# S5 states stored by place in a block, the S5 recurrence on VectorE alone, and two gate items moved into the RWKV groups

## What is computed

```python
def rwkv7_scan(r, w, k, v, kk, a):
    def step(state, xs):
        r_t, w_t, k_t, v_t, kk_t, a_t = xs
        sa = jnp.einsum('bhvk,bhk->bhv', state, -kk_t)
        state = (state * w_t[:, :, None, :] + sa[..., None] * (kk_t * a_t)[:, :, None, :]
                 + v_t[..., None] * k_t[:, :, None, :])
        return state, jnp.einsum('bhvk,bhk->bhv', state, r_t)
...
    # s5_branch: 64 groups of 64 complex states, s_t = a * s_(t-1) + bu_t
    bu_re = jnp.einsum('gpc,blgc->blgp', bb_re, ug)
    bu_im = jnp.einsum('gpc,blgc->blgp', bb_im, ug)
    _, _, s_re, s_im = lax.associative_scan(combine, (a_re_t, a_im_t, bu_re, bu_im), axis=1)
    y = jnp.einsum('gcp,blgp->blgc', c_re, s_re) - jnp.einsum('gcp,blgp->blgc', c_im, s_im)
...
    # second_block
    gates = jax.nn.sigmoid(gate_logits.astype(jnp.float32).reshape(bsz, seq, N_BRANCH, D_MODEL)
                           + gate_b[i].astype(jnp.float32))
    merged = jnp.sum(gates * branch_proj, axis=2)
```

## Time and profile before

| | us |
|---|---|
| median of 3 runs | 4223.11 (4216.96 to 4227.99) |
| the profiled execution | 4227.98 |
| its span | 4226.1 |
| TensorE busy | 3696.7 (87%) |
| VectorE busy | 2460.8 (58%) |
| ScalarE busy | 1190.7 (28%) |
| GpSimd busy | 477.2 (11%) |
| mean granted TensorE clock | 0.937 |

### The profile page before, as it was taken

The page is one execution under the profiler, slowest core; times in us unless marked ns, Lnnn a source line. Parts: engine busy times, 40 slices in busy tenths (PEclk is TensorE's granted clock), DMA queues, the critical chain, the costliest instruction groups (busy, mean ns, idle before and its releaser), DMA issues. The chain is left out here.

```text
span 4226.1 us, 47590 instructions
## 1 busy us (share of the span) xinstructions
PE 3696.7 (87%) x19527; PEld 2904.3 (69%) x19527; DVE 2460.8 (58%) x3027; ACT 1190.7 (28%) x1252; POOL 477.2 (11%) x713
## 2 busy tenths in 40 slices
PE   2599868899999999999999699787977777999888
PEld 1475547789999999888888587486835774444336
DVE  7665668579777644555555545655445445993224
ACT  1223223334444443434334332213311002000003
POOL 1011101000100000000000000020001110992000
PEclk9999869899999999999999898898988888999999
DMA  7866327356777676766667452105451005553553
GB/s 269 301 225 201 117 74 301 138 187 199 259 252 251 247 248 219 242 241 243 245 240 247 150 199 87 45 1 209 159 181 35 1 6 150 145 159 119 184 206 122
DMA packets 246293, 750.71 MB, mean 178 GB/s; under 512 B 31264, under 2 KB 42612, under 8 KB 210368
## 3 DMA queue, kind: packets, MB, share of 16 engines
q1 hardware_dynamic: 217008, 645.44, 44.5%
q0 software_dynamic: 29072, 102.25, 6.9%
HBM read 692.29 MB, written 54.75 MB: 177 GB/s over the span
## 5 line engine op out<-in xcount | busy, mean ns | idle before, releaser
L1860 DVE TENSOR_TENSOR expert_w_low<-expert_w,expert_w_high 128x2048 fp32r<-128x2048 f32 x256 | 586.6, 2292 | 556.2 <-ACT expert_w_high L2152 555.7
L2152 ACT ACTIVATE expert_w_high<-expert_w 128x2048 fp32r<-128x2048 f32 x256 | 489.4, 1912 | 433.7 <-PE bank L2141 410.5
L2082 PE MATMUL bank<-h_high,expert_w_high 128*128 128x256 f32 x2048 | 583.7, 285 | 9.3 <-DVE expert_w_low L1860 8.2
L2083 PE MATMUL bank<-h_low,expert_w_high 128*128 128x256 f32 x2048 | 580.5, 283 | 0.0
L2084 PE MATMUL bank<-h_high,expert_w_low 128*128 128x256 f32 x2048 | 580.4, 283 | 0.0
L281 DVE TENSOR_TENSOR weights_low<-weights,weights_high 128x1024 fp32r<-128x1024 f32 (+2 forms) x280 | 328.8, 1176 | 324.4 <-ACT weights_high L268 322.0
L268 ACT ACTIVATE weights_high<-weights 128x1024 fp32r<-128x1024 f32 (+2 forms) x280 | 284.9, 1021 | 678.5 <-PE bank L305 424.1
L2082 PEld LDWEIGHTS bank<-h_high,expert_w_high 128*128 128x128 f32 x2048 | 394.0, 192 | 10.2 <-DVE expert_w_low L1860 8.8
L2139 PE MATMUL bank<-expert_w_high,gated_acts_high 128*128 128x512 f32 x1024 | 398.3, 389 | 0.0
L2140 PE MATMUL bank<-expert_w_low,gated_acts_high 128*128 128x512 f32 x1024 | 398.3, 389 | 0.0
L2141 PE MATMUL bank<-expert_w_high,gated_acts_low 128*128 128x512 f32 x1024 | 398.3, 389 | 0.0
(11 more groups left out here) (670 smaller groups left out, 5803.5 us busy)
## 6 DMA issues: line engine op xcount, KB each, us to landing
expert_w<-in_peer_u_dram SPq DMA_DIRECT2D x128, 1024.0 KB, 5.9
expert_w<-in_peer_v_dram SPq DMA_DIRECT2D x128, 1024.0 KB, 5.0
weights<-in_w_in_dram SPq DMA_DIRECT2D x84, 1024.0 KB, 9.8
s_gates_w<-in_w_in_dram SPq DMA_DIRECT2D x80, 512.0 KB, 3.6
ada_ring<-in_ada_w_dram SPq DMA_DIRECT2D x64, 512.0 KB, 5.0
weights<-in_w_out_dram SPq DMA_DIRECT2D x32, 1024.0 KB, 11.6
weights<-in_w_branch_dram SPq DMA_DIRECT2D x48, 512.0 KB, 6.0
mod_mid_ring<-in_ada_w_dram POOLq DMA_DIRECT2D x32, 512.0 KB, 6.5
```

The costliest lines, as they stand in the source:

```text
L1860: dve.tensor_tensor(wl[:, n % RING, :], w_sb[:, n % RING, :], wh[:, n % RING, :], ALU.subtract).then_inc(wl_ready, 1)
L2082: pe.matmul(o, uh[:, b, k, :], acts.h[:, k, :], start=(k == 0), stop=False)
L2083: pe.matmul(o, uh[:, b, k, :], acts.l[:, k, :], start=False, stop=False)
L2152: act.activation(wh[:, n % RING, :], w_sb[:, n % RING, :], ACT.Copy).then_inc(wh_ready, 1)
```

## The change

The S5 states are stored by place: `S[f]` is now [128, 16 places, 32 tiles, 16 blocks], so that one place of all tiles is 512 neighbouring elements. TensorE reads the input tokens in that order (every 16th column of `s5_u_columns`), and reads the states back in token order for the outputs (every 512th element). VectorE runs the recurrence for all 32 tiles; GpSimd has no work in the block. Carries are added to four tiles at a time. The pair of gate items 2 and 3 leaves the second S5 block, which now has seven, and goes into the four RWKV groups: of each group's four units one stands after the eight banks of products, one after the first product of c = 0, one after the second product of c = 0, and one after the first product of c = 1. In that block the inverse's copies use banks 4 and 5 alone, and the gate items banks 6 and 7. SyncE loads the two items' weights (8 MB) in that block, which had no loads. The `s5_in` item that follows is unchanged.

```diff
-        self.n = 0
+        self.n, self.copies = 0, m.to_act
...
-                bank = m.to_act.take(pe)
+                bank = self.copies.take(pe)
                 for u in range(4 * half, 4 * half + 4):
                     mm = pe.matmul(bank[:, (u % 4) * P:(u % 4 + 1) * P], self.M[:, u, :], self.T[:, u, :], start=True, stop=True)
-                m.to_act.put(mm)
+                self.copies.put(mm)
...
+        self.ring = m.to_act
...
+GATES_BESIDE_RWKV = 2
+
+GROUP_PARTS = (1, (1, 1), (1, 0))
...
+        s5_jobs = [(io["w_in_2"][0], SU0 + c * CHUNK, None, ACT.Copy, s5_dram[c]) for c in range(4)]
+        rwkv_jobs = s5_jobs[0:3] + gate_jobs(io, gates_dram, GATES_BESIDE_GDN, GATES_BESIDE_GDN + GATES_BESIDE_RWKV) + s5_jobs[3:4]
+        beside = Beside(m, st, ctx, "s5_in", whole, rwkv_jobs)
...
+            inv.copies = BankRing(m.banks[4:6], m.sem("rwkv_copies_filled"), m.sem("rwkv_copies_emptied"))
+            beside.ring = BankRing(m.banks[6:8], m.sem("rwkv_beside_filled"), m.sem("rwkv_beside_emptied"))
...
+                @block.sync
+                def _(sp):
+                    beside.on_sp(sp, GATES_BESIDE_RWKV)
...
+                        if n % 2:
+                            beside.on_act(act)
...
+                        beside.on_pe(pe, GROUP_PARTS[0])
                         inv.on_pe(pe)
...
+                            beside.on_pe(pe, GROUP_PARTS[1 + c][0])
                             pe.wait_ge(x_ready, step + 1)
                             bank = m.to_dve.take(pe)
                             for u, h in hs:
                                 mm = pe.matmul(bank[ps, u * RN:(u + 1) * RN], TT_[:, u, ps], xu[:, 0, u * RN:(u + 1) * RN],
                                                start=True, stop=True)
                             m.to_dve.put(mm)
+                            beside.on_pe(pe, GROUP_PARTS[1 + c][1])
...
+        beside.ring = m.to_act
...
-S5_AT_DVE = 22
-S5_CARRY_TILES = 2
+S5_CARRY_TILES = 4
...
-    cut = [s[:, i0:i1, :].rearrange("p i (b j) -> p i b j", j=S5_BLOCK) for s in S]
     for j in range(1, S5_BLOCK):
-        s5_accumulate(eng, C, [s[:, :, :, j] for s in cut], [spread(x[:, i0:i1], S5_BLOCKS) for x in a],
-                      [s[:, :, :, j - 1] for s in cut], temps([n, S5_BLOCKS]))
+        s5_accumulate(dve, C, [s[:, j, :, :] for s in S], [spread(x, S5_BLOCKS) for x in a],
+                      [s[:, j - 1, :, :] for s in S], temps([S5_TILES, S5_BLOCKS]))
 
     for f in range(2):
-        C(eng.tensor_copy(carry[f][:, i0:i1, 1:], cut[f][:, :, 0:S5_BLOCKS - 1, S5_BLOCK - 1]))
+        C(dve.tensor_copy(carry[f][:, :, 1:], S[f][:, S5_BLOCK - 1, :, 0:S5_BLOCKS - 1]))
     for b in range(2, S5_BLOCKS):
-        s5_accumulate(eng, C, [x[:, i0:i1, b] for x in carry], [w[:, i0:i1, S5_BLOCK - 1] for w in pw],
-                      [x[:, i0:i1, b - 1] for x in carry], temps([n]))
-
-    for i in range(i0, i1, S5_CARRY_TILES):
-        q = S5_CARRY_TILES
-        powers = [bass.AP(tensor=w.tensor, offset=w[:, i:i + q, :].offset,
-                          ap=[list(w.ap[0]), [S5_BLOCK, q], [0, S5_BLOCKS - 1], [1, S5_BLOCK]]) for w in pw]
-        s5_accumulate(eng, C, [s[:, i:i + q, S5_BLOCK:].rearrange("p i (b j) -> p i b j", j=S5_BLOCK) for s in S],
-                      powers, [spread(x[:, i:i + q, 1:], S5_BLOCK) for x in carry], temps([q, S5_BLOCKS - 1, S5_BLOCK]))
+        s5_accumulate(dve, C, [x[:, :, b] for x in carry], [w[:, :, S5_BLOCK - 1] for w in pw],
+                      [x[:, :, b - 1] for x in carry], temps([S5_TILES]))
+
+    q, n = S5_CARRY_TILES, S5_BLOCKS - 1
+    for i in range(0, S5_TILES, q):
+        powers = [view(w[:, i, 0:1], [[1, S5_BLOCK], [S5_BLOCK, q], [0, n]]) for w in pw]
+        carries = [view(x[:, i, 1:2], [[0, S5_BLOCK], [S5_BLOCKS, q], [1, n]]) for x in carry]
+        s5_accumulate(dve, C, [s[:, :, i:i + q, 1:] for s in S], powers, carries, temps([S5_BLOCK, q, n]))
         yield i
...
-        jobs = gate_jobs(io, gates_dram, GATES_BESIDE_GDN, BRANCHES * (D // CHUNK))
+        jobs = gate_jobs(io, gates_dram, GATES_BESIDE_GDN + GATES_BESIDE_RWKV, BRANCHES * (D // CHUNK))
...
-        S = arrays_of(m.weights.buf[0], 1, [S5_TILES, T]) + arrays_of(m.weights.buf[1], 1, [S5_TILES, T])
+        S = [arrays_of(m.weights.buf[f], 1, [S5_BLOCK, S5_TILES, S5_BLOCKS])[0] for f in range(2)]
+
+        def by_place(ap):
+            return ap.rearrange("p (b j) -> p j b", j=S5_BLOCK)
+
+        def places(ap):
+            return ap.rearrange("p (j b) -> p j b", j=S5_BLOCK)
...
-                            mm = pe.matmul(bank[:, f * T:(f + 1) * T], BT[q, i // 4, f, :], uT[q, i // 4, :], start=True, stop=True)
+                            mm = pe.matmul(places(bank[:, f * T:(f + 1) * T]), BT[q, i // 4, f, :], by_place(uT[q, i // 4, :]),
+                                           start=True, stop=True)
                         ring.put(mm)
...
-                            if i < S5_AT_DVE:
-                                pe.wait_ge(s_dve, i // S5_CARRY_TILES + 1)
-                            else:
-                                pe.wait_ge(s_pool, (i - S5_AT_DVE) // S5_CARRY_TILES + 1)
+                            pe.wait_ge(s_dve, i // S5_CARRY_TILES + 1)
                             o = bank[(i % 4) * 32:(i % 4 + 1) * 32, (i // 4 % 2) * T:(i // 4 % 2 + 1) * T]
                             for f in range(2):
-                                mm = pe.matmul(o, CT[:, i // 4, f, (i % 4) * 32:(i % 4 + 1) * 32], S[f][:, i, :],
-                                               start=(f == 0), stop=(f == 1))
+                                mm = pe.matmul(o.rearrange("p (b j) -> p b j", j=S5_BLOCK), CT[:, i // 4, f, (i % 4) * 32:(i % 4 + 1) * 32],
+                                               S[f][:, :, i, :].rearrange("p j b -> p b j"), start=(f == 0), stop=(f == 1))
                         m.to_dve.put(mm)
...
-                        act.activation(S[0][:, i, :], bank[:, 0:T], ACT.Copy)
-                        m.to_act.free(act.activation(S[1][:, i, :], bank[:, T:2 * T], ACT.Copy))
+                        act.activation(S[0][:, :, i, :], places(bank[:, 0:T]), ACT.Copy)
+                        m.to_act.free(act.activation(S[1][:, :, i, :], places(bank[:, T:2 * T]), ACT.Copy))
...
-                @block.gpsimd
-                def _(pool):
-                    L = m.pool_chain.on(pool)
-                    pool.wait_ge(bu_act, 1)
-                    pool.wait_ge(bu_ready, 1)
-                    for _i in s5_scan(pool, L, S5_AT_DVE, S5_TILES, S, a, pw, carry, tmp_pool):
-                        pool.drain().then_inc(s_pool, 1)
...
-                        dve.tensor_copy(S[0][:, i, :], bank[:, 0:T])
-                        m.to_dve.free(dve.tensor_copy(S[1][:, i, :], bank[:, T:2 * T]))
-                    dve.drain().then_inc(bu_ready, 1)
+                        dve.tensor_copy(S[0][:, :, i, :], places(bank[:, 0:T]))
+                        m.to_dve.free(dve.tensor_copy(S[1][:, :, i, :], places(bank[:, T:2 * T])))
                     V(dve.engine_nop())
                     dve.wait_ge(bu_act, 1)
-                    for _i in s5_scan(dve, V, 0, S5_AT_DVE, S, a, pw, carry, tmp_dve):
+                    for _i in s5_scan(dve, V, S, a, pw, carry, tmp_dve):
```

More of the change, by code:

```diff
@@ L2275, in on_act @@
             for half in range(2):
-                bank = self.m.to_act.get(act)
-                self.m.to_act.free(act.activation(self.h(self.X, half), self.bank3(bank), ACT.Copy))
+                bank = self.copies.get(act)
+                self.copies.free(act.activation(self.h(self.X, half), self.bank3(bank), ACT.Copy))
                 act.drain().then_inc(self.x, 1)
@@ L2752, with stage_rwkv @@
 LN_EPS = 64e-5
-def stage_rwkv(nc, m, io, st, whole, cols, s5_dram):
+def stage_rwkv(nc, m, io, st, whole, cols, s5_dram, gates_dram):
     with ExitStack() as ctx:
@@ L2775, in stage_rwkv @@
         chunk_ind = m.sb(ctx, "chunk_indicator", [P, 2])
-        beside = Beside(m, st, ctx, "s5_in", whole, [(io["w_in_2"][0], SU0 + c * CHUNK, None, ACT.Copy, s5_dram[c]) for c in range(4)])
+        s5_jobs = [(io["w_in_2"][0], SU0 + c * CHUNK, None, ACT.Copy, s5_dram[c]) for c in range(4)]
+        rwkv_jobs = s5_jobs[0:3] + gate_jobs(io, gates_dram, GATES_BESIDE_GDN, GATES_BESIDE_GDN + GATES_BESIDE_RWKV) + s5_jobs[3:4]
+        beside = Beside(m, st, ctx, "s5_in", whole, rwkv_jobs)
         def part(i, tt):
@@ L3409, in stage_s5 @@
             tmp_dve = [m.sb(c2, f"s5_tmp_dve{q}", [P, size])[:, :] for q in range(4)]
-            tmp_pool = [m.sb(c2, f"s5_tmp_pool{q}", [P, size])[:, :] for q in range(4)]
             a = [consts[:, f, :] for f in range(2)]
-            bu_ready, bu_act, s_dve, s_pool, y_ready = (m.sem("s5_" + s) for s in ("bu_by_dve", "bu_by_act", "states_dve", "states_pool", "y_ready"))
+            bu_act, s_dve, y_ready = (m.sem("s5_" + s) for s in ("bu_by_act", "states_dve", "y_ready"))
             with nc.Block() as block:
```

17 lines of the change are left out of this document (8 added, 9 removed).

## The result

Ten runs of the changed kernel have a median of 4204.36 us beside 4222.85 for ten of the kernel before, 18.5 us less. One of the ten, the profiled one, was disturbed and took 16.5 ms; the other nine have a median of 4202.01, and the ratio 0.995, interval [0.9938, 0.9962], is theirs. That is further from 1 than the 0.3% that can be told. The forecast was 4182 (4168 to 4205): faster was right, but by about half of the 41 us that I expected, and 4204.36 lies in the range by 0.6 us. The profile after is that of the first experiment (e1), the same kernel unaltered: 4194.25 us, ratio 0.9929 [0.9916, 0.9943]. The eleventh experiment ran it a third time: 4197.16, 0.9941 [0.9927, 0.9954].

The account below looks back on a forecast made before the run. TensorE's nine gate items were taken to bound the second S5 block, a to-and-fro chain the RWKV groups. -61.5 + 31.8 + 0.5 - 12 = -41.2 us gave 4186.8 profiled, 4182 as median; range 4168 to 4205.

Parts of the forecast that it names:

- The two items that leave S5: Second S5 block: TensorE's list sets the end, so two gate items of 30.73 us fewer save 61.5 us.
- VectorE in time: Second S5 block: VectorE alone finishes the scan in 190.9 us, 22 us ahead of TensorE, at no cost.
- VectorE the bound: Rival, S5 block: operand pattern, not GpSimd, slows the recurrence; 1.46 us an operation, kernel at 4255; 3%.
- The groups: RWKV groups: 31.8 us paid for units outside the long waits, 0.5 for drains, 12 returned by the clock.
- The clock: RWKV groups: filled waits raise TensorE's granted clock; three quarters of the possible gain, 12 us, was taken.
- full return: RWKV groups: upper end of the clock gain, 15.8 us, from 2.0 a group and 3.9 in two groups.
- the long second group: RWKV groups: second lasts 5.9 us more than third, 2 from more state products, 3.9 from low clock.
- each group 5 us longer: Expected sign in the RWKV groups: each of the four lasts 5 us longer than before.
- the 8 us that I had named as a sign of being wrong: RWKV groups: the prediction is wrong if a group gets longer by 8 us or more.
- How TensorE reads the states: S5 input and output products: reading single elements far apart was taken to cost 0.
- the rival that I gave 14%: S5 products: scattered reads end the overlap; outputs 20.6 us more (4203, 8%), inputs 17.6 too (4220, 6%).
- the last of my signs of being wrong: S5 input and output products: the prediction is wrong if either takes over 12 us.

Follow-up runs that it names:

- e5: Changed kernel with S5 states stored tile by tile as before and VectorE alone on all 32 tiles: 4184.05 us, ratio 0.99.
- e6: Changed kernel with each group's four units moved: two in the long wait, one in the first chunk, one before the second chunk's first product: 4187.98 us, ratio 0.9911.
- e8: Changed kernel with all four units of each group in the long wait and none in the chunks: 4205.84 us, ratio 0.9946.
- e4: Changed kernel with TensorE reading inputs in order and states in runs of 16; VectorE's copies and last step do the permuting: 4187.5 us, ratio 0.9907.
- e11: Changed kernel run again, unaltered: 4197.16 us, ratio 0.9941 against the kernel before.
- e3: Changed kernel with the S5 scan of before, states tile by tile and shared by VectorE and GpSimd: 4208.05 us, ratio 0.9961.
- e7: Changed kernel with the edits of e4 and e6, and the next item's first weights loaded while the groups run: 4164.6 us, ratio 0.9853.
- e9: e7 with a third gate item in the RWKV groups, six units a group: 4154.95 us, ratio 0.9841.
- e10: e9 with S5 states tile by tile, VectorE alone on them, and without the edit of e4: 4187.68 us, ratio 0.9912.
- e2: Changed kernel with the two gate items back in S5 and none in the groups: 4238.39 us, ratio 1.0032.

## Why the prediction was right or wrong

**The two items that leave S5**, -61.5: 59.9 came. Right, by the stage.

**VectorE in time**: right, and the scan was quicker than summed, 175.8 us for 190.9. Powers 6.2 (7), recurrence 77.9 (81.6), carry additions 72 (81.6); the last was called an upper bound. The rival "VectorE the bound" was weighed with a wrong picture: operands far apart do cost VectorE, 1.03 against 0.69 us, and the change took just this away (e5). It would have been 1.46 had all of before's step come from it. The repeated coefficient, which I named as the cause, is in e1 too, at 0.69 us.

**The groups**, +31.8 + 0.5 - 12 = +20.3: measured +20.8, but that is luck, since two of its terms were off by about 7 us, one each way. The two items kept TensorE busy for 66.1 us, not 59.0 + 0.5, since units stood in stretches of low clock too. Of this 26.8 lay in waits (idle 53.2 before, 26.4 after), where the forecast had 27.2. That leaves 39.3 paid for 32.3. The clock gave back 66.1 - 26.8 - 20.8 = 18.5 instead of 12, more than the 15.8 that I had called full return. About half of it came in the inverse, behind the long wait (118.5 us busy in the four groups before, 109.6 after), where I had 8.0. The other half came in the chunks, where I had 7.8 at most and had misread the cause of the long second group: its chunks have as many records as those of the first (224), and e6's chunks, at the full clock and with two units each, are busy for 19.9 and 20.7 us. So 0.7 of the 5.3 us between them is work and the rest clock; I had put 2 us down to more products. e8 shows that the two halves are separate: there the inverse gained as much (109.4), but the chunks lost 7.7 us (61.6 busy before, 69.3), so that 63.3 us of items, 23.3 of them in waits, lengthen the groups by 37.6 and only 2.4 come back. It is the units in the chunks that bring back the chunks' clock. This is from one execution of e8, a slow one. Nor was each group 5 us longer as told: they are 6.5, 2.0, 8.5 and 3.7 us longer. The third passes the 8 us that I had named as a sign of being wrong; there is a bias in it, and its chunks had no low clock to win back.

**How TensorE reads the states**, taken at 0: this is the step that failed. I argued from whole gate products that a record needs an element only every 0.85 ns, and that four streams at once would do. It cost 10.8 us, 4.0 at the inputs and 6.8 at the outputs: the mechanism of the rival that I gave 14%, at 10.8 of its 38.2 us. A record of the outputs became twice as long and not four times, and at the inputs VectorE's copies had set the pace before, so that part of the loss is hidden. Both products take over 12 us, the last of my signs of being wrong: the time came in, this part of the mechanism did not. e4 shows that nothing else did it. The Trainium skill had spoken against the change here ("Advanced Engine Details and Errata", SBUF Cachelines: each access to another line pays), and the trace agrees in sign: 0.110 us a record of the outputs for single elements apart, 0.056 for runs of 16. I should have taken a value between the ends rather than the lower end.

**The clock in the S5 block's first part**, not in the sum: +4.7 us in e1, 0 in e11, 4.2 to 4.5 in e3, e7 and e8, and within 0.5 of none in e4, e5, e6, e9 and e10. It differs between executions of one kernel (e1, e11), so I take it for chance; neither kernel without the items in the groups (before, e2) showed it, but two profiles say little. What makes TensorE's clock return early or late behind the 21 us wait for the S5 rows stays open.

**The sum**: 4186.8 was forecast for the profiled execution and 4194.25 measured. Change by change: reads +10.8, clock chance +4.7, items +1.6, groups +0.5, other small terms; and -10.6 from stretches that the change doesn't touch (7.1 ahead of the groups, 3.5 behind the outputs; the profiled execution before lay 4.9 us over its median). Without these last, the forecast would have missed by 18 us. The medians of the other two comparisons, 4204 and 4197, miss 4182 by 22 and 15. Why three comparisons of one kernel have medians from 4194 to 4204 was not settled beyond that.

## What to carry to other kernels

A new order of data in SBUF is paid or earned at every reader: count the engine with no time to spare first. Here VectorE's gain of 42 us was idle time, TensorE's loss of 10.8 was not; let the reader take runs (16 elements did) and do the permuting in operations that read PSUM anyway and that nothing waits for. Filling waits with independent matmuls pays twice where a low clock follows the waits, but it depends on the place: first the longest waits, then one unit between short ones; the same 16 units made these groups 262, 275 or 292 us long in the profiled executions. Read the clock of each stretch by itself: in e8 filling one wait brought back the clock behind that one alone. And when work is taken out from under a cover, try one piece more: the layout that seven items didn't need gave 33 us with six.

## What the runs showed of the hardware

- Single fp32 elements as TensorE's moving operand, narrow products overlapped: 0.111 us for a record of 256 columns with elements 64 bytes apart (inputs), 0.110 with 2 KB (outputs); in order the outputs take 0.056. The stride made no difference, runs of 16 elements at 2 KB were free. The inputs in order took 0.081, paced by VectorE's copies.
- VectorE's tensor_tensor on 512 fp32 elements 64 bytes apart: 1.03 to 1.07 us, on neighbours 0.69. Its copies out of PSUM read 64 bytes apart took 0.41 us for 256 elements, as those in order do.
- Before, eight far-apart operations on 352 elements took 8.05 us beside GpSimd; alone they take 8.02 on 512 (e5), so that GpSimd beside them cost a factor of about 1.4 to 1.5 per element (an estimate, since an operation also has a fixed part). The Trainium skill ("SBUF — State Buffer", Who interferes with whom) says that a VectorE instruction with two SBUF inputs contends with a GpSimd instruction that reads SBUF; these two steps agree.
- The granted clock in the chunks, one profiled execution each: 1.00, 0.78, 1.00, 0.79 before, with every wait open; 0.71, 0.84, 0.71, 0.85 in e8, with the long wait full and the short ones open; 1.00 in all four in e6, with two units a group in the long wait and two in the chunks.
